# A streaming encoder layer on one core: new order of the first block, mixer steps placed to end at place 60, S5 output stored by quarters, low halves of the down weights on GpSimd

## The reference

```
h   = rmsnorm(x, norm_mix);  z = h @ w_in          # xl | gl | us, 512 columns each
xc  = causal_conv(xl) (4 taps);  r, ig = sigmoid(xc @ wa + ba), sigmoid(xc @ wx + bx)   # 8 heads of 64
a   = exp(-8 r softplus(-lambda));  hl = scan(a, sqrt(1 - a^2) * ig * xc)
y_lru = hl * gelu(gl)
ys  = S5(us): 32 groups, 64 complex states each, plus d * us;  g = gelu(ys)
y_ssm = g * sigmoid(g @ w_glu + b_glu)
x   = x + [rmsnorm(y_lru) | rmsnorm(y_ssm)] @ w_out
h2  = rmsnorm(x, norm_ffn);  x = x + (silu(h2 @ w_gate) * (h2 @ w_up)) @ w_down   # 2816 wide
y   = rmsnorm(x, norm_final)
```

## Time and profile before

| | us |
|---|---|
| median of 3 runs | 2478.4 |
| profiled execution: time | 2483.81 |
| its span, first to last instruction | 2482.0 |
| TensorE busy | 2244.3 (90%), mean granted clock 0.945 |
| TensorE weight loads busy | 2173.5 (88%) |
| VectorE busy | 1549.7 (62%) |
| ScalarE busy | 1110.4 (45%) |
| GpSimd busy | 408.3 (16%) |
| DMA | 322.84 MB, 130 GB/s over the span |

### The profile page before, as it was taken

One profiled execution on the slowest core, in us unless ns is written; L12 is line 12 of the kernel. 1 busy time (PEld: TensorE's weight loads), 2 busy tenths in 40 slices (PEclk: granted clock), 3 DMA queues, 4 the chain that ended last, 5 costly groups with the idle time before them and its releaser, 6 DMA issues.

```text
span 2482.0 us, 30507 instructions
## 1 busy us (share of the span) xinstructions
PE 2244.3 (90%) x11746; PEld 2173.5 (88%) x11746; DVE 1549.7 (62%) x2601; ACT 1110.4 (45%) x1481; POOL 408.3 (16%) x483
## 2 busy tenths in 40 slices
...
GB/s 146 105 124 176 47 121 118 125 152 164 147 101 107 171 107 154 160 164 113 112 136 154 138 130 203 94 119 110 175 140 152 145 128 111 104 145 119 110 123 52
DMA packets 191073, 322.84 MB, mean 130 GB/s; under 512 B 82896, under 2 KB 121104, under 8 KB 190800
## 3 DMA queue, kind: packets, MB, share of 16 engines
...
HBM read 296.39 MB, written 26.53 MB: 130 GB/s over the span
## 4 chain that ended last, share of the span: by engine, by line
PE 78%; DVE 4%; SPq 3%; ACT 2%; POOL 2%; issue 2%; DMA 1%; POOLq 0%; DVEq 0%; ACTq 0%
PE acc L787 25%; PE acc L789 24%; PE acc L788 24%; SPq L449 3%; PE acc L863 1%; PE acc L864 1%; DVE rstd L1041 1%; PE acc L873 1%; POOL tmp L511 1%; PE acc L843 1%; DVE w_hl L924 1%; PE acc L853 1%; DMA g_dram<-u 1%; DVE act_hl L924 1%; POOL s5p L536 0%
## 5 line engine op out<-in xcount | busy, mean ns | idle before, releaser
L787 PE MATMUL acc<-act_hl,w_hl 128*128 128x416 f32 x2640 | 951.8, 361 | 59.0 <-DVE act_hl L924 55.3
L789 PE MATMUL acc<-act_hl,w_hl 128*128 128x416 f32 x2640 | 940.6, 356 | 0.0
L788 PE MATMUL acc<-act_hl,w_hl 128*128 128x416 f32 x2640 | 938.1, 355 | 0.0
L924 DVE TENSOR_TENSOR w_hl<-w_raw,w_hl 128x1024 fp32r<-128x1024 f32 x440 | 545.3, 1251 | 115.0 <-ACT w_hl L611 113.4
L787 PEld LDWEIGHTS acc<-act_hl,w_hl 128*128 128x128 f32 x2640 | 507.6, 192 | 77.9 <-issue 54.6
L788 PEld LDWEIGHTS acc<-act_hl,w_hl 128*128 128x128 f32 x2640 | 507.9, 192 | 8.8 <-issue 3.1
L789 PEld LDWEIGHTS acc<-act_hl,w_hl 128*128 128x128 f32 x2640 | 506.4, 192 | 1.8
L611 ACT ACTIVATE w_hl<-w_raw 128x1024 fp32r<-128x1024 f32 x440 | 454.8, 1051 | 91.0 <-DMA w_raw<-in_w_ffn 45.7
L924 DVE TENSOR_TENSOR x_acc<-x_acc,acc 128x416 f32<-128x416 f32 x480 | 272.5, 585 | 228.6 <-PE acc L789 222.9
L511 POOL TENSOR_TENSOR tmp<-tmp 128x416 f32<-128x416 f32 x135 | 169.7, 1257 | 1193.2 <-ACT tmp L619 1184.6
L787 PE MATMUL acc<-ff_hl,w_hl 128*128 128x416 f32 x880 | 315.1, 358 | 24.8 <-DVE x_acc L924 22.0
...
## 6 DMA issues: line engine op xcount, KB each, us to landing
...
```

What stands on the lines that cost most here:

```text
L787: pe.matmul(out, w(0), x(0), start=first, stop=False)
L788: pe.matmul(out, w(0), x(1), start=False, stop=False)
L789: return pe.matmul(out, w(1), x(0), start=False, stop=last)
L924: return v.tensor_tensor(out, x, y, op)
```

## The change

1. *Order of block 0.* `FIRST` is written anew, in smaller steps. x comes in two halves (`x_half`), units 0 and 1 are loaded before the parameters; `w0` is three steps between the squares; `tb` is split in `tb` (GpSimd), `ts` (ScalarE) and `tr` (rho and stores), and `tb` 0 no longer waits for `rho_done` and `bb_done`; `pq` is ScalarE's part of `pb`, earlier; `gl` units come before `xl`; c1t and bmt have two tiles each; the store of c1t moves from step `c1` to step `ck`. The S5 steps start before `xl` 2, 3 and stand between the steps of the LRU.
2. *Steps split.* `zst` is the z store, out of `xl` 0; `cv` the conv, out of `xl`; `bx` the product, out of `ga`.
3. *S5 output by quarters.* `gst` j stores quarter j (8 DMAs of 16 partitions, into a `g_dram` laid out by heads), `gld` j loads it with one DMA, `gs` j splits one chunk.
4. *Places.* `MIXER` is written anew; h2 is at places 58 to 60 instead of 63 and 64.
5. *Down units.* Their low halves are made by GpSimd, at the same point of the order as before (place of the step two ahead, before the step's own work), counted by `wd_lo`; VectorE skips them.

The core of the diff (small renamings, and the LRU state code that only moves under a new step name, are left out):

```diff
-         (25, ("us", 0)), (25, ("us", 1)), (26, ("us", 2)), (26, ("us", 3)), (27, ("xl", 0)), (28, ("xl", 1)),
...
+         (25, ("us", 0)), (25, ("us", 1)), (26, ("us", 2)), (26, ("us", 3)), (27, ("xl", 0)), (27, ("zst", 0)),
+         (28, ("cv", 0)), (28, ("xl", 1)), (28, ("zl", 0)), (28, ("ga", 0)), (28, ("gl", 0)),
+         (29, ("bx", 0)), (29, ("cv", 1)), (29, ("ga", 1)), (29, ("gl", 1)), (29, ("gl", 2)),
+         (30, ("bx", 1)), (30, ("la", 0)), (30, ("gl", 3)), (30, ("s5", 0)), (33, ("lb", 0)), (33, ("s5", 1)), (33, ("lc", 0)),
+         (34, ("ld", 0)), (34, ("s5", 2)), (34, ("xl", 2)), (35, ("ld", 1)), (35, ("s5", 3)),
+         (36, ("cv", 2)), (36, ("xl", 3)), (36, ("ga", 2)), (36, ("s5", 4)), (39, ("bx", 2)), (39, ("cv", 3)), (39, ("ga", 3)),
+         (39, ("s5", 5)), (40, ("bx", 3)), (40, ("la", 1)), (40, ("s5", 6)), (40, ("s5", 7)), (41, ("lb", 1)), (41, ("lc", 1)),
+         (41, ("s5", 8)), (41, ("gst", 0)), (42, ("ld", 2)), (42, ("s5", 9)), (45, ("ld", 3)), (45, ("s5", 10)),
+         (45, ("gld", 0)), (45, ("gst", 1)), (45, ("nls", 0)), (46, ("s5", 11)), (46, ("s5", 12)), (46, ("nls", 1)),
+         (47, ("s5", 13)), (47, ("s5", 14)), (47, ("gld", 1)), (47, ("gst", 2)), (48, ("gs", 0)), (48, ("s5", 15)), (48, ("nl", 0)),
+         (49, ("s5", 16)), (49, ("s5", 17)), (49, ("gst", 3)), (49, ("gld", 2)), (51, ("ml", 0)), (51, ("ml", 1)), (51, ("gs", 1)),
+         (51, ("gld", 3)), (52, ("gs", 2)), (52, ("gs", 3)), (52, ("glu", 0)), (53, ("glu", 1)), (53, ("ns", 0)),
+         (54, ("ms", 0)), (54, ("ms", 1)), (54, ("out", 0)), (54, ("out", 1)), (54, ("out", 2)), (54, ("out", 3)),
+         (55, ("out", 4)), (55, ("out", 5)), (55, ("out", 6)), (55, ("out", 7)), (57, ("sq2", 0)), (57, ("n2", 0)),
+         (58, ("h2", 0)), (59, ("h2", 1)), (60, ("h2", 2)), (60, ("h2", 3))]
...
+FIRST = [("x", 0), ("pa", 0), ("sq1", 0), ("w0", 0), ("sq1", 1), ("w0", 1), ("sq1", 2), ("w0", 2), ("sq1", 3), ("tb", 0),
+         ("pq", 0), ("n1", 0), ("h1", 0), ("h1", 1), ("h1", 2), ("h1", 3),
+         ("us", 0), ("ts", 0), ("tr", 0), ("tb", 1), ("pb", 0), ("us", 1), ("pc", 0), ("us", 2), ("c1", 0), ("us", 3),
+         ("ts", 1), ("tr", 1), ("tb", 2), ("zst", 0), ("c1", 1), ("gl", 0), ("ck", 0), ("c1", 2), ("gl", 1), ("ck", 1), ("c1", 3),
+         ("gl", 2), ("ck", 2), ("bm", 0), ("ts", 2), ("tr", 2), ("tb", 3), ("gl", 3), ("ck", 3), ("bm", 1), ("bt", 0),
+         ("xl", 0), ("bm", 2), ("bt", 1), ("kt", 0), ("cv", 0), ("bm", 3), ("bt", 2), ("xl", 1), ("ts", 3), ("tr", 3), ("bt", 3),
+         ("zl", 0), ("pl", 0), ("ga", 0), ("bx", 0), ("cv", 1), ("ga", 1), ("bx", 1), ("s5", 0), ("la", 0), ("s5", 1), ("lb", 0),
+         ("s5", 2), ("lc", 0), ("s5", 3), ("ld", 0), ("s5", 4), ("ld", 1), ("xl", 2), ("s5", 5), ("cv", 2), ("s5", 6), ("xl", 3),
+         ("ga", 2), ("s5", 7), ("bx", 2), ("cv", 3), ("gst", 0), ("s5", 8), ("ga", 3), ("bx", 3), ("s5", 9), ("la", 1), ("gld", 0),
+         ("s5", 10), ("lb", 1), ("gst", 1), ("s5", 11), ("lc", 1), ("s5", 12), ("gs", 0), ("ld", 2), ("s5", 13), ("ld", 3),
+         ("gld", 1), ("s5", 14), ("gst", 2), ("s5", 15), ("gs", 1), ("nls", 0), ("s5", 16), ("gld", 2), ("s5", 17), ("gst", 3),
+         ("nls", 1), ("nl", 0), ("gs", 2), ("gld", 3), ("ml", 0), ("ml", 1), ("gs", 3), ("glu", 0), ("glu", 1), ("ns", 0),
+         ("ms", 0), ("ms", 1)] + [("out", d) for d in range(KD)] + [("sq2", 0), ("n2", 0)] + [("h2", i) for i in range(4)]
...
-        g_dram = nc.dram_tensor("g_dram", (2, L, HG, G, C5), F32).ap()
+        g_dram = nc.dram_tensor("g_dram", (2, KL, GE, HG, L, C5), F32).ap()
...
-            load_x(0)
+            for h in range(2):
+                sp.dma_start(x_acc[0][:, 4 * h:4 * h + 4, :], a["x"][0][:, 4 * h:4 * h + 4, 0:T]).then_inc(x_half[h], 16)
+            for u in range(2):
+                load_unit(u)
...
+                elif kind == "gst":
+                    wait_evacuated(sp, ("y5", b, 4 * j + 1))
+                    wait_evacuated(sp, ("y5", b, 4 * j + 2))
+                    wait_evacuated(sp, ("y5", b, 4 * j + 3))
+                    if b >= 2:
+                        sp.wait_ge(ys_in[j], 16 * (b - 1))
+                    for s in range(L):
+                        sp.dma_start(g_dram[b % 2][j, :, :, s, :].rearrange("g h c -> h g c"),
+                                     u5[s * HG:(s + 1) * HG, j * GE:(j + 1) * GE, :]).then_inc(g_st[j], 16)
+                elif kind == "gld":
+                    sp.wait_ge(z_st, 16 * (b + 1))
+                    sp.wait_ge(g_st[j], 16 * L * (b + 1))
+                    sp.dma_start(zs[:, j].rearrange("p s c -> p (s c)"), g_dram[b % 2][j].rearrange("g h s c -> (g h) (s c)"))\
+                      .then_inc(ys_in[j], 16)
...
+                u = PLACE[step] + LEAD_LO if step in PLACE else NU
+                if u < NU and SRC[u][0] == "dn":
+                    po.wait_ge(w_hi, u + 1)
+                    slot = w_hl[u % RING]
+                    po.tensor_tensor(slot[:, 1, :], w_raw[u % RING][:], slot[:, 0, :].bitcast(F32), ALU.subtract).then_inc(wd_lo, 1)
...
-                elif kind == "c1":
+                elif kind == "ck":
+
                     po.wait_ge(c1_done, j + 1)
...
-                        po.wait_ge(rho_done, 1)
-                        po.wait_ge(bb_done, 1)
...
-                    pe.wait_ge(w_lo, UNIT[step] + (2 if kind == "dn" else 1))
+                    if kind == "dn":
+                        pe.wait_ge(wd_lo, DOWN_BEFORE[UNIT[step]] + 2)
+                    else:
+                        pe.wait_ge(w_lo, UNIT[step] - DOWN_BEFORE[UNIT[step]] + 1)
...
             def weight_lo(u):
+                if SRC[u][0] == "dn":
+                    return
```

More of the change, by code:

```diff
@@ L122 @@
 NU = len(SRC)
+DOWN_BEFORE = [sum(k == "dn" for k, _, _ in SRC[:n]) for n in range(NU + 1)]
 PREP = {}
@@ L411, in _ @@
                     sp.wait_ge(z_st, 16 * (b + 1))
-                    sp.wait_ge(g_st, 16 * KL * b) if b else None
+                    if b:
+                        for e in range(KL):
+                            sp.wait_ge(g_st[e], 16 * L * b)
                     for s in range(L):
@@ L514, in _ @@
             made_n = [0]
-            for kind, b, j in STEPS:
+            for step in STEPS:
+                kind, b, j = step
+                u = PLACE[step] + LEAD_LO if step in PLACE else NU
[3 more added lines that the diff above has]
+                    po.tensor_tensor(slot[:, 1, :], w_raw[u % RING][:], slot[:, 0, :].bitcast(F32), ALU.subtract).then_inc(wd_lo, 1)
                 if kind in ("sq1", "nls", "nfs"):
@@ L540, in _ @@
                     for (p0, p1), (c0, c1) in cols:
-                        step = 1 if p1 - p0 == c1 - c0 else c1 - c0 - 1
-                        ins = po.tensor_tensor(s5x[:, s, :, p0:p1], s5p[:, s, 0, :, c0:c1:step], s5p[:, s, 1, :, c0:c1:step],
+                        by = 1 if p1 - p0 == c1 - c0 else c1 - c0 - 1
+                        ins = po.tensor_tensor(s5x[:, s, :, p0:p1], s5p[:, s, 0, :, c0:c1:by], s5p[:, s, 1, :, c0:c1:by],
                                                ALU.subtract)
@@ L651, in _ @@
                 elif kind == "w0":
-                    for u in range(LEAD_HI):
-                        weight_hi(u)
+                    weight_hi(j)
                 elif kind == "ck":
+                    if j == 1:
+                        act.wait_ge(zero_st, 16 * KL)
                     if j >= 2:
@@ L674, in _ @@
                 elif kind in ("sq1", "nls", "nfs"):
-                    if (kind, j) == ("sq1", 0):
-                        act.wait_ge(x_in[b % 2], 16 * (b // 2 + 1))
+                    if kind == "sq1" and b == 0 and j % 2 == 0:
+                        act.wait_ge(x_half[j // 2], 16)
+                    elif (kind, j) == ("sq1", 0):
+                        act.wait_ge(x_in[b % 2], 16 * ((b + 1) // 2))
                     if (kind, j) == ("nfs", 0):
@@ L1115, in _ @@
                     angles()
-                elif kind == "w0":
-                    for u in range(LEAD_LO):
-                        weight_lo(u)
+                elif kind == "w0" and j < LEAD_LO:
+                    weight_lo(j)
                 elif kind == "pb":
@@ L1148, in _ @@
                     h_lo_split(kind, b, H_PARTS[j][-1])
[L1149 removed]
+                elif kind == "cv":
                     if (b, j) == (0, 0):
```

123 lines of the change are left out of this document (52 added, 71 removed), and 13 rows, old and new, of tables (FIRST, MIXER).

## The result

The kernel after the change takes 2666.0 us (median of 4 runs, 2665.1 to 2669.5) where the kernel before takes 2478.4: ratio 1.076, 95% interval 1.074 to 1.078. It is **7.6% slower**. The 2478.4 is the median of three runs; a fourth, of 3758.6 us, stands far apart and is left out. The forecast was 2454 us with a range of 2398 to 2500: it had the sign wrong, and the result lies far outside the range.

A forecast was written before the change was run, and what follows sets the result against it. First part bound by a chain of latencies (sine tables, loads, S5 steps), blocks by TensorE, busy 97% and more. 2483.8 - 50 (first part) + 26 (four blocks) = 2459.8, 2454 us on the median's scale; range 2398 to 2500.

The forecast's parts named there:

- The first part: Stretch before any feed-forward work, 346.8 us: first glu unit at 225.5 instead of 275.7, gain 50 us (30 to 70).
- 3.5 us to land before the next turn may write: Sine table loop of the first block: time for each turn's stores to land, 3.5 us.
- The new wait of `c1` 2: First block: c1 2 waits for the c1t0 store behind turn 2; VectorE idle from about 65 to 82 us.
- the net of +6.5 us a block: Steady blocks: 21.6 us added less 15 removed, +26 us in four blocks (bounds -9 to +17 a block).
- Added (1), (3) and (4): New TensorE waits a block: before ga 1 and ga 3 8.3 us together, before ns 3.9, at out 0 3.
- Removed, glu: Old glu waits, 9.4 us by unit starts, go; low half 3 some 4.7 late, 6.4 with clock; gain 3.
- Removed, the reciprocal and h2: Reciprocal of 2.75 us no longer before down pairs' adds, twice; h2 never late; gain 6 us a block.
- Added (2), GpSimd: GpSimd's low half takes 2.3 us; TensorE waits 1.6 in each of down 4 to 7, 6.4 a block.
- Removed, VectorE's relief: VectorE loses 8 low halves of 1.25 us in the S5 stretch, 10 us; 6 taken back (0 to 9).
- rival B: Chance 0.07: GpSimd's low halves hold VectorE, +18 us a block, first part gives 30; 2546 us.
- A: Rival, chance 0.28: the new order hides its new waits, blocks come out even, first part gives 65 us; 2413 us.
- C and D: Rivals on the first part: gives only 25 us, 2479, chance 0.12; gives 15 us more, 2439, chance 0.08.

The follow-up runs named there:

- the four kernels: Changed kernel with low halves on VectorE 2587.8 us, with old places 2500.9, with both 2427.4; kernel before with low halves on GpSimd 2549.0.
- `s5_conv`: Changed kernel with low halves on VectorE and old places from gs to h2 (2508.5 us), convs 1 and 3 right behind their xl: 2457.0 us.
- `s5_la`: Changed kernel with low halves on VectorE and old places from gs to h2 (2508.5 us), la 1 behind S5 steps 6 and 7: 2482.2 us.
- `gs_n2`: Changed kernel with old places and VectorE's low halves (2427.4 us), n2 one place earlier, gs 0 to 3 at new places, glu unmoved: 2404.4 us.
- `end_new`: Changed kernel, low halves on VectorE, old places except gs, glu, ns, ms, out, sq2, n2 and h2 at the new ones: 2491.8 us.
- `low_dve`: Changed kernel with the low halves of the down units back on VectorE, all else as changed: 2587.8 us.
- `gp_quiet`: Changed kernel with old places, GpSimd making the low halves of down pairs 0 to 3 and 8 to 10 only: 2462.5 us.
- `gp_dummy`: Changed kernel with old places, VectorE making all low halves, GpSimd subtracting a spare tile at the same places for nobody: 2461.5 us.

## Why the prediction was wrong

**The first part: right in kind, 18 us too good.** Forecast 50 us, measured 32.4 (35.3 with old places and VectorE's low halves), near the low bound of 30. The first S5 matmul came at 155.7 us, not 137. The step that was sized too short is a turn of the sine table: "3.5 us to land before the next turn may write". That is what the trace before has (median 3.6 us from issue to landing); after, the median is 5.9. GpSimd's timeline after has the waits for the landings:

```profile
51.82 4.63 POOL L598 TENSOR_TENSOR tq<-jrow,tau 128x432 f32<-128x432 f32 x1 [4.78 <-DMA t_dram<-tq]
...
79.79 0.91 POOL L598 TENSOR_TENSOR tq<-jrow,tau 128x432 f32<-128x432 f32 x1 [5.90 <-DMA t_dram<-tq]
...
112.47 1.08 POOL L598 TENSOR_TENSOR tq<-jrow,tau 128x432 f32<-128x432 f32 x1 [5.59 <-DMA t_dram<-tq]
```

Idle of 4.8 to 5.9 us stands in front of each of these turns, and the contended turn (51.82 to 68.6) took 16.8 us, not 13. So turn 3 started at 112.5 instead of 100, and the chain from its end to the first S5 matmul took 30 us instead of 25. The new wait of `c1` 2 is there as forecast (VectorE waits 25.3 us for the store of c1t0, TensorE stands 28.0 between two units; the forecast had 15 to 17 on VectorE). The S5 stretch, from the first S5 matmul to the first glu unit, took 77.5 us (155.7 to 233.2) where the text has 137 to 225.5, 88.5: 11 better. From there to the first gate unit it took 81.2 where the text kept 71, since the first glu unit now begins on the first quarter and then waits for its other operands (2.16 and 5.12 us), much of it at the lower clock: it takes 16.4 us for 4.51. What the forecast took for the end of the stretch was only the start of that unit. Its 12.5 us from the last gelu to there were also added wrongly: the terms given (3.8, 2, 0.4, 2 and 2) make 10.2, and the load's 2 us to land (1.9 before, for small loads) is 4.4 for the large ones after.

**Steady blocks: the step that failed is the net of +6.5 us a block.** Measured +52 on average. What failed in it are the price of the added waits, two waits that it did not see (`la` 1, and what stands behind h2), and the low halves of GpSimd outside the S5 stretch, put at nothing. By the four kernels the places cost 40 us a block where its terms for them (15.2 added, 9 removed) net 6, and GpSimd 18 to 20 where its terms (6.4 added, 6 removed) net nothing. Part by part:

*Added (1), (3) and (4), the new places.* The waits were right: 4.04, 3.97, 3.89 and 2.96 us for 4.1, 4.1, 3.9 and 3. The sum of them was taken as their price. `s5_conv` and `s5_la` measured the price: 1.6 and 1.4 us per microsecond of wait, because TensorE's clock is at its lower level for the first microseconds behind a wait of 4 us (0.50 from 1091.95 to 1096.00, above). The forecast had used this itself, once, on the credit side ("a second one and 3 us of half clock" behind the old glu wait), and left it out of everything that it added. With 1.6 the 15.1 us of added waits would have been 24; that is 9 us a block, a part of what is missing and not all of it. Waits of 2 us are not free either: the down pair behind the 2.07 us at 842.53 took 10.8 us, where a pair with no wait before it takes 9.1; the one behind 2.06 us at 903.23 took 9.3. `out` 0 also has a second wait, 1.10 us at 1213.39, that the forecast did not have.

*A wait that was missed.* `la` 1 in front of S5 steps 6 and 7. ScalarE's timeline after, before the v5 matmuls of 1091.95:

```profile
1085.54 1.16 ACT L745 ACTIVATE tmp<-tmp,small 128x416 f32<-128x416 f32 x2
1086.70 1.28 ACT L747 ACT_TABLE_LOAD   x1
...
1090.25 1.28 ACT L757 ACT_TABLE_LOAD   x1
1091.55 0.41 ACT L757 ACTIVATE u<-acc 128x104 f32<-128x104 f32 x2
```

The gelu of 0.4 us, which empties the PSUM tile that v5 needs, stands behind six activations of `la` 1 and two table loads, 6.0 us. 4.70 us of wait a block, 6.6 in all. The text counted the S5 steps themselves and what VectorE had to do, but not the order on ScalarE across a moved step.

*Removed, glu.* This term held. The forecast had 4.7 us of wait, 6.4 us with the clock, and a gain of 3; in block 1 glu waits 1.57 and 2.81 us, and glu 0 costs 6.4 us above its unit, where before it costs some 9.8: 4.90 us of wait, 1.06 behind it and the rest clock. With old places and the quarters the two waits are 0.51 and 1.68 us, and `gs_n2` has none: more was to be had by early gs and an unmoved glu.

*Removed, the reciprocal and h2, "gain 6".* The two waits for `x_acc` (1.65 us at ns and 2.1 at n2) are gone from block 1 as forecast, but a new wait took their place. A down pair behind h2 starts with a wait of its own, and its 48 matmuls take 11.7 us where such a pair takes 9.1:

```profile
1284.95 0.58 DVE L948 TENSOR_TENSOR ff_hl<-f_g,ff_hl 128x416 fp32r<-128x416 f32 x1
...
1285.63 0.68 PE L808 MATMUL acc<-ff_hl,w_hl 128*128 128x416 f32 x1 [4.43 <-issue]
```

Since h2 now comes four to five places earlier, VectorE has its products in the queue (1270.14 to 1285) ahead of the hidden product that this pair waits for; in `end_new` and `low_dve` it is a low half, and the wait 3.57 and 3.56 us. "h2 is never late" holds, but what stands behind h2 is.

*Added (2), GpSimd.* "The 14 other down halves lie where TensorE has no wait, and are worth nothing" and "GpSimd queues nothing else that is late" both failed: `gp_quiet` has 35 us there. The forecast looked for what is behind S5 steps and overlooked the sums of squares, which wait on ScalarE in the same queue. Its 6.4 us a block in the S5 pairs was right as a wait (6.7), and low as a price: 74 - 35 = 39 us for the rest, 9.8 a block. (Its own numbers, 2.1 + 1.45 + 2.3 against 4.5, give 1.35 us a pair and not 1.6.)

*Removed, VectorE's relief, "I take 6 back".* Moving the low halves off VectorE never gained, in any of the three pairs of kernels. And most of the relief is not there: with the same places, block 1 has 296.3 us of VectorE in `low_dve` and 289.9 in the kernel after, 6.4 less, where 22 subtractions of 1.22 to 1.25 us, 27 us of work, have left it. Some 21 us came back as longer instructions beside GpSimd's: this is the mechanism of rival B, and it was real. In block 1 of the kernel after a conv beside one GpSimd subtraction takes 4.19 us where the same three instructions took 2.03:

```profile
984.32 2.03 DVE L951 SCALAR_TENSOR_TENSOR tmp<-xl,vec,tmp 128x416 f32<-128x416 f32 x3
...
1046.68 2.41 POOL L531 TENSOR_TENSOR w_hl<-w_raw,w_hl 128x1024 fp32r<-128x1024 f32 x1
1046.71 4.19 DVE L951 SCALAR_TENSOR_TENSOR tmp<-xl,vec,tmp 128x416 f32<-128x416 f32 x3
```

The Trainium skill, SBUF — State Buffer, section "Who interferes with whom", says that a VectorE instruction with two SBUF inputs contends with a GpSimd instruction that reads SBUF, and that the port pair they share is an exclusive lock. The trace agrees: 4.19 - 2.03 = 2.16 us, close to the 2.41 of GpSimd's instruction.

**The rivals.** B was nearest, 2546 with a chance of 0.07, and its mechanism holds; but by `gp_dummy` VectorE and GpSimd's queue together are worth 34 us, not 72. That its number was the nearest is luck, and it is still 120 us short: its own two terms (the first part at 30, and +18 a block) hold no wait behind `la` 1, nothing for h2 and no price of the clock. None of the rivals had the main term, new places that cost more than their waits: A had those waits hidden, and C and D were about the first part alone. The gain that the change did bring, first block and quarters, 54 us, is near the forecast's 50, but for the first part alone it was 32 to 35; the 160 us of the places and the 74 of GpSimd hid it.

**What stays open.** Of the end half of the places (64 us) the waits are read from the trace (1.58, 2.79, 3.90, 2.95, 1.78 and 3.57 us in block 1 of `end_new`), but not taken away one at a time. Nor is it known where the 15 us come from by which the two halves fall short of the whole, and no kernel tried a first block whose table stores land earlier.
